# Six modulation blocks moved from TensorE to GpSimd in a two-block transformer kernel

## The reference

```python
def adaln(cond, w_mod, b_mod):
    m = jax.nn.silu(cond) @ w_mod + b_mod
    return _split(m, (D_MODEL, D_MODEL, D_MODEL))
...
sh_l, sc_l, ga_l = adaln(c, w_mod[layer], b_mod[layer])
sh_c, sc_c, ga_c = adaln(c_ctx, w_mod[layer], b_mod[layer])
h_lat = rms_norm(x_lat, g_pre[layer]) * (1 + sc_l[:, None]) + sh_l[:, None]
```

## Time and profile before

| | |
|---|---|
| runs (3) | 2313.47 us median, 2302.77 to 2314.18 |
| profiled execution | 2318.67 us, its span 2316.9 us |
| granted clock, mean | 0.985 of full |
| PE busy | 2250.4 us (97%) |
| DVE busy | 1409.2 us (61%) |
| ACT busy | 877.6 us (38%) |
| POOL busy | 10.4 us |
| ring loads | 154 x 2 MB, 7.7 us to landing |

### The profile page before, as it was taken

One profiled execution on the slowest core, in us unless ns is written; L12 is line 12 of the kernel. 1 busy time (PEld: TensorE's weight loads), 2 busy tenths in 40 slices (PEclk: granted clock), 3 DMA queues, 4 the chain that ended last, 5 costly groups with the idle time before them and its releaser, 6 DMA issues.

```text
span 2316.9 us, 34330 instructions
## 1 busy us (share of the span) xinstructions
PE 2250.4 (97%) x14514; PEld 1974.6 (85%) x14514; DVE 1409.2 (61%) x2026; ACT 877.6 (38%) x994; POOL 10.4 (0%) x23
## 2 busy tenths in 40 slices
PE   7999999999999999999999999999999997999997
PEld 7997999799889879997997568888788857999976
DVE  5556876755465568767556455666666257665564
ACT  4333474334333333652443332222434242443442
POOL 0000000000000000000000000000000000000000
PEclk9999999999999999999999999999999998999998
DMA  6555545646454544555554421111212342232331
GB/s 243 208 220 196 187 182 188 230 170 231 182 200 183 218 182 184 183 197 219 212 192 172 164 109 73 73 62 48 73 37 74 117 146 73 93 126 74 138 118 55
DMA packets 26552, 349.39 MB, mean 151 GB/s; under 512 B 2912, under 2 KB 3168, under 8 KB 5728
## 3 DMA queue, kind: packets, MB, share of 16 engines
q1 hardware_dynamic: 23888, 336.49, 39.2%
q0 software_dynamic: 2512, 10.72, 1.4%
HBM read 346.14 MB, written 1.05 MB: 150 GB/s over the span
## 4 chain that ended last, share of the span: by engine, by line
PE 87%; DVE 6%; ACT 2%; DMA 2%; DVEq 1%; issue 1%; ACTq 0%; SPq 0%
PE banks L703 12%; PE banks L708 12%; PE banks L704 12%; PE banks L792 9%; PE banks L868 9%; PE banks L926 5%; PE banks L927 5%; PE banks L930 5%; PE banks L944 2%; PE banks L940 2%; PE banks L941 2%; PE banks L1105 2%; PE banks L1106 2%; PE banks L696 2%; PE banks L1103 2%; PE banks L752 2%
## 5 line engine op out<-in xcount | busy, mean ns | idle before, releaser
L1808 DVE TENSOR_TENSOR w_lo<-ring,w_hi 128x2048 fp32r<-128x2048 f32 x290 | 662.6, 2291 | 468.9 <-ACT w_hi L1312 465.0
L1312 ACT ACTIVATE w_hi<-ring 128x2048 fp32r<-128x2048 f32 x290 | 554.8, 1917 | 705.5 <-PE banks L708 485.3
L703 PE MATMUL banks<-x_hi,w_hi 128*128 128x256 f32 x2208 | 520.4, 278 | 1.4 <-ACT arena L1406 1.4
L704 PE MATMUL banks<-x_lo,w_hi 128*128 128x256 f32 x2208 | 519.5, 277 | 0.0
L703 PEld LDWEIGHTS banks<-x_hi,w_hi 128*128 128x128 f32 x2208 | 415.5, 188 | 1.8 <-ACT arena L1406 1.8
L704 PEld LDWEIGHTS banks<-x_lo,w_hi 128*128 128x128 f32 x2208 | 415.5, 188 | 0.0
L708 PE MATMUL banks<-x_hi,w_lo 128*128 128x256 f32 x2208 | 298.3, 278 | 0.0
L708 PEld LDWEIGHTS banks<-x_hi,w_lo 128*128 128x128 f32 x2208 | 273.3, 188 | 0.4 <-DVE w_lo L1808 0.4
L1343 ACT ACTIVATE arena<-banks 128x512 f32<-128x512 f32 (+3 forms) x164 | 79.2, 498 | 443.1 <-PE banks L930 200.5
L926 PE MATMUL banks<-x_hi,w_hi 128*128 128x512 f32 (+1 forms) x656 | 237.6, 374 | 0.0
L927 PE MATMUL banks<-x_lo,w_hi 128*128 128x512 f32 (+1 forms) x656 | 228.8, 361 | 0.0
(11 more groups left out here) (322 smaller groups left out, 2800.3 us busy)
## 6 DMA issues: line engine op xcount, KB each, us to landing
ring<-weights SPq DMA_DIRECT2D x154, 2048.0 KB, 7.7
arena<-mods SPq DMA_DIRECT2D x5, 2048.0 KB, 12.2
bcast<-lnrows POOLq DMA_DIRECT2D x12, 512.0 KB, 4.9
arena<-hy_consts POOLq DMA_DIRECT2D x1, 1152.0 KB, 7.5
xrow<-x SPq DMA_DIRECT2D x1, 1024.0 KB, 4.9
arena<-hy_consts POOLq DMA_DIRECT2D x1, 1024.0 KB, 10.5
xrow<-ctx_rows POOLq DMA_DIRECT2D x1, 1024.0 KB, 5.3
out<-xrow SPq DMA_DIRECT2D x2, 512.0 KB, 2.7
```

Source lines behind the costliest of these rows:

```text
L703: nc.tensor.matmul(out, hi[:, k, t * P:(t + 1) * P], x_h[:, k, :], start=k == 0, stop=False)
L704: nc.tensor.matmul(out, hi[:, k, t * P:(t + 1) * P], x_l[:, k, :], start=False, stop=False)
L1312: nc.scalar.activation(hi, raw, ACT.Copy).then_inc(w_hi_done, 1)
L1808: v.tensor_tensor(lo, raw, hi.bitcast(F32), ALU.subtract).then_inc(w_lo_done, 1)
```

## The change

Blocks 5 to 10 leave the ring and TensorE's rows. In three of the four FFNs GpSimd loads two of them, one after the other, into `mod_w`. It multiplies the eight 128x512 pieces by the condition columns (a scalar for each partition) and adds them up in a new tile `vacc`, so that 128 partial sums per output column remain. In the turn behind the FFN, TensorE adds over the partitions: eight fp32 matmuls per block, with a piece of `vacc` as the weights and one column of ones moving, straight into the form of columns. The two steps `mod_copy` and `mod_columns` fall away for these blocks. SP's load of the next early block into `mod_w` moves from behind down block 0 to behind down block 2 and waits for GpSimd's count `vmod_done`. `vtmp` and `vacc` lie in parts of the arena that are free in an FFN.

```diff
-    return up(0) + down(0) + mix + up(1) + down(1) + (mod(5, 6, 7) if l == DEPTH - 1 else [])
+    return up(0) + down(0) + mix + up(1) + down(1)
...
-    blocks += [(("ey", j), 2) for j in range(4)] + [(("mod", m), 0) for m in (8, 9, 10)]
+    blocks += [(("ey", j), 2) for j in range(4)]
...
+FFN_MODS = {(0, 0): (5, 6), (0, 1): (7, 8), (1, 0): (9, 10)}
...
     def mod_use(n):
-        for kind in ("mrow", "mcol"):
-            uses[kind, n] = (4, count[4])
-            count[4] += 1
+        if 3 * l + n < 5:
+            for kind in ("mrow", "mcol"):
+                uses[kind, n] = (4, count[4])
+                count[4] += 1
+        if n % 2 == 0:
+            for bank, m in enumerate(FFN_MODS.get((l, n // 2), ()), 5):
+                uses["vcol", m] = (bank, count[bank])
+                count[bank] += 1
...
-                if l < DEPTH and (kind, *rest) in (("down", 0, 0), ("up", 1, 0), ("down", 1, 0)):
-                    m = 3 * l + (("down", 0, 0), ("up", 1, 0), ("down", 1, 0)).index((kind, *rest))
+                if l < DEPTH and (kind, *rest) in (("down", 0, 2), ("up", 1, 0), ("down", 1, 2)):
+                    m = 3 * l + (("down", 0, 2), ("up", 1, 0), ("down", 1, 2)).index((kind, *rest))
...
                     if kind == "up":
                         sp.wait_ge(m_done, 4 * l + 4)
+                    else:
+                        sp.wait_ge(S2["vmod_done"], 2 * (l + l + rest[0]) + 2)
                     sp.dma_start(mod_w, mods[m].rearrange("p (k n) -> p k n", k=KT)).then_inc(S2["mod_in"], 16)
...
+            def modulation(l, f, slot, k):
+
+                i = 2 * l + f
+                w = mod_w[:, k, :]
+                if k == 0:
+                    pool.wait_ge(S2["cond_done"], 1)
+                    if i:
+                        filled(pool, *mod_key("mcol", FFN_ORDER[2 * i - 2 + slot]))
+                    pool.wait_ge(S2["vmod_in"], 16 * (2 * i + slot + 1))
+                    for c in range(2):
+                        nc.gpsimd.tensor_scalar(vacc[:, slot, c, :], w, cond[:, k, c:c + 1], None, ALU.mult)
+                else:
+                    for c in range(2):
+                        nc.gpsimd.tensor_scalar(vtmp[:, c, :], w, cond[:, k, c:c + 1], None, ALU.mult)
+                    nc.gpsimd.drain()
+                    for c in range(2):
+                        nc.gpsimd.tensor_tensor(vacc[:, slot, c, :], vacc[:, slot, c, :], vtmp[:, c, :], ALU.add)
+                if k < KT - 1:
+                    nc.gpsimd.drain()
+                else:
+                    nc.gpsimd.drain().then_inc(S2["vmod_done"], 1)
...
+                    if (l, n / 2) in FFN_MODS:
+                        for slot, m in enumerate(FFN_MODS[l, n // 2]):
+                            if slot:
+                                pool.wait_ge(S2["vmod_done"], 2 * (2 * l + n // 2) + 1)
+                            elif l + n == 0:
+                                filled(pool, 0, "layer", "up", 0, 1, 0)
+                            else:
+                                filled(pool, *mod_key("mrow", 3 * l + n - 1))
+                            pool.dma_start(mod_w, mods[m].rearrange("p (k n) -> p k n", k=KT))\
+                                .then_inc(S2["vmod_in"], 16)
+                            for k in range(KT):
+                                modulation(l, n // 2, slot, k)
...
+                if n % 2 == 0 and (l, n // 2) in FFN_MODS:
+                    for slot, v_mod in enumerate(FFN_MODS[l, n // 2]):
+                        pe.wait_ge(S2["vmod_done"], 2 * (2 * l + n // 2) + slot + 1)
+                        b = take(pe, *mod_key("mcol", v_mod))
+                        for t in range(4):
+                            for c in range(2):
+                                mm = nc.tensor.matmul(banks[:, b, 2 * t + c:2 * t + c + 1],
+                                                      vacc[:, slot, c, t * P:(t + 1) * P], ones[:, 0:1],
+                                                      start=True, stop=True)
+                        mm.then_inc(full[b], 1)
```

More of the change, by code:

```diff
@@ L94, in layer_blocks @@
     down = lambda f: [(("down", f, q), 2 if 2 * q + 1 < DOWN_HALVES else 1) for q in range(W2_BLOCKS)]
-    mod = lambda *numbers: [(("mod", m), 0) for m in numbers]
     mix = []
@@ L131 @@
 BLOCK_OF, HALF_OF, HALVES = number_blocks()
+FFN_MODS = {(0, 0): (5, 6), (0, 1): (7, 8), (1, 0): (9, 10)}
+FFN_ORDER = [m for pair in FFN_MODS.values() for m in pair]
 MOD_BLOCK = {key[2]: n for key, n in BLOCK_OF.items() if key[1] == "mod"}
@@ L158, with plan_layer @@
 SLOT0_LAST = max(h for h, s in HI_SLOT.items() if s == 0 and h < FIRST_HALVES)
-def plan_layer(last):
+def plan_layer(l):
     uses, count, pair = {}, [0] * 8, [0]
+    last = l == DEPTH - 1
     def pair_use(*key):
@@ L239, in plan_banks @@
         "start": (1, in_turn(*[("turn", b, b) for b in range(4)])),
-        **{("layer", l): (1, plan_layer(l == DEPTH - 1)) for l in range(DEPTH)},
+        **{("layer", l): (1, plan_layer(l)) for l in range(DEPTH)},
         "even": (1, in_turn(
-            *[("pre", k, k) for k in range(KT)], *[(kind, m, 2 * m - 10) for m in (6, 7) for kind in ("mrow", "mcol")],
+            *[("pre", k, k) for k in range(KT)],
             *[("gg", w, h, 7) for w in range(2) for h in range(2)],
@@ L251, in plan_banks @@
         "even_y": (1, in_turn(*[("y", h, r, ((0, 1, 2, 6), (3, 4, 5, 7))[h][r]) for h in range(2) for r in range(4)])),
-        "odd": (1, in_turn(*[(kind, m, m - 8) for m in (8, 9) for kind in ("mrow", "mcol")],
-                           *[("pre", k, k) for k in range(KT)], ("mrow", 10, 2), ("mcol", 10, 2), ("gif", 3),
+        "odd": (1, in_turn(*[("pre", k, k) for k in range(KT)], ("gif", 3),
                            ("ct", 6), ("em", 7))),
@@ L360, in build @@
         mod_w = arena[:, top[0]:top[0] + BLK].rearrange("p (k n) -> p k n", k=KT)
+        vtmp = arena[:, FT * SEQ * 2 + 1024:FT * SEQ * 2 + 2048].rearrange("p (c n) -> p c n", c=2)
+        vacc = arena[:, top[0] + BLK:top[0] + BLK + 2048].rearrange("p (s c n) -> p s c n", s=2, c=2)
         th_g_at, th_g = arena_at + 4 * top[0], part(4096, 2 * KT, SEQ)
@@ L513, in mod_key @@
         def mod_key(kind, m):
+            if m in FFN_ORDER:
+                return FFN_ORDER.index(m) // 4, "layer", "vcol", m
             if m < 6:
                 return m // 3, "layer", kind, m % 3
-            return 0, "even" if m < 8 else "odd" if m < 11 else "tail", kind, m
+            return 0, "tail", kind, m
         half_keys = {h: key for key, h in HALF_OF.items()}
@@ L970, in features_ready @@
                 return lambda k: pe.wait_ge(S2["x2_split"], KT * layer + k + 1)
-            mod_row(5, range(KT))
             pe.wait_ge(S2["f_done"], 1)
@@ L984, in _ @@
                                            for t in range(2)], done=b)
-                if p == 1:
-                    mod_columns(5)
             turn_all("even", erow)
-            mod_row(6, range(KT))
-            mod_row(7, range(KT))
-            mod_columns(6)
             def even_gains(w, h):
@@ L1011, in _ @@
                         .then_inc(full[b], 1)
-                    if i == 0 and t == 0:
-                        mod_columns(7)
                     if i == 1 and t == 0:
@@ L1177, in _ @@
                     even_half(j, side)
-            mod_row(8, range(KT))
-            mod_row(9, range(KT))
-            mod_columns(8)
-            mod_columns(9)
             turn_all("odd", yrow)
-            mod_row(10, range(KT))
             pe.wait_ge(S2["gw_split"], 1)
@@ L1892, in ffn @@
                         mod_add(3 * l + 2 * f - 1)
+                        for m in FFN_MODS[0, 1] if (l, f) == (1, 0) else ():
+                            mod_add(m)
                 for q in range(DOWN_HALVES - 2):
@@ L1992, in _ @@
                         mod_add(3 * l)
+                        for m in FFN_MODS[l, 0]:
+                            mod_add(m)
                     after(l, "xb", h, 1)
@@ L2133, in _ @@
             weights_lo(HALF_OF[DEPTH, "hy", 0, 1])
-            for m in (6, 7):
-                mod_add(m)
             def hy(i, c):
@@ L2356, in _ @@
             prenorm(1, yrow)
-            for m in (8, 9):
-                mod_add(m)
-            v.drain()
             pre_gain(1)
@@ L2529, in block @@
         return m.reshape(KT, P, n).transpose(1, 0, 2).reshape(P, BLK)
-    def modulation(*numbers):
-        out.extend(block(i["w_mod_2"][m // 6][:, 512 * (m % 6):512 * (m % 6 + 1)]) for m in numbers)
     def units(m):
@@ L2565, in weight_blocks @@
         ffn(1)
-    modulation(5, 6, 7)
     return out
 def early_modulation(i):
-    return np.stack([i["w_mod_2"][0][:, 512 * m:512 * (m + 1)].reshape(KT, P, 512).transpose(1, 0, 2).reshape(P, BLK)
-                     for m in range(5)])
+    return np.stack([i["w_mod_2"][m // 6][:, 512 * (m % 6):512 * (m % 6 + 1)].reshape(KT, P, 512)
+                     .transpose(1, 0, 2).reshape(P, BLK) for m in range(11)])
```

(2 more changed lines are left out.)

13 lines of the change are left out of this document (2 added, 11 removed).

## The result

| | before | after |
|---|---|---|
| runs beside each other | 2308.40 us (2302.77 to 2328.62, 6 runs) | 2347.64 us (2344.81 to 2350.27, 6 runs) |
| profiled execution, its span | 2318.67 us, 2316.9 us | 2345.66 us, 2343.6 us |
| granted clock, mean | 0.985 | 0.971 |

The change makes the kernel slower: the ratio is 1.0157, with an interval of 1.0133 to 1.018. The profiled spans differ by 26.7 us, the medians by 39.2 us; the profiled execution of before lies 10 us above the median of its runs here, which accounts for most of the difference.

The account below looks back on a forecast made before the run. TensorE, busy 97% of the span, was taken to bound the kernel. Terms -8.0 - 8.5 - 9.0 + 7.2 = -18.3 us, from an adjusted 2313.5, gave 2295 us if FFNs ran as before; range 2285 to 2334.

Parts of the forecast that it names:

- The step that failed: GpSimd in the FFNs: 60 operations of 128x512 at 1.0 us each, 60 us, within the 1.63 us each allowed in the first.
- upper bound of 1.3 us: GpSimd's average operation if each operand and the result cost a memset's pass: multiply 1.1 us, add 1.6.
- Rival 1: FFNs: GpSimd and DVE hold each other up, 46 us lost, 28 us slower in all, 2341 us; chance 0.26.
- The deadline: SP's queue: SP must pass its wait for GpSimd by 161 in the first FFN, 600.5 in the second.
- The second block: Modulation matmuls removed from TensorE at the second block's layers: gains of 8.0, 8.5 and 9.0 us.
- block 5: Start of the second block: row matmuls of 6.96 us and columns of 1.05 us go, all moves forward, -8.0 us.
- blocks 6 and 7: Before the first Hyena tile: 9.2 us won, 7.5 after reduced clock, plus 1.0 for later columns: -8.5 us.
- Blocks 8 to 10: From their first row matmuls to the first mLSTM head tile: -9.0 us, bounds 6.5 and 11.5.
- Rival 3: Second block: removed work was mostly cover as TensorE waits for ACT; gain only 9 us, 2304 us; chance 0.09.
- The turns: Three turns behind FFNs get 16 one-column matmuls each, 3.73 us, less 4.0 us of covered waits: +7.2 us.
- a slower DVE alone does no harm: FFN up phases: w_lo is ready several us before its use, so slower DVE costs nothing by itself.
- Rival 2: Milder holding: operations take 1.6 to 1.85 us, only the first FFN loses, up to 13 us; middle 2303; chance 0.19.

Follow-up runs that it names:

- the merged kernel: Each GpSimd pair of 512 columns merged into one instruction of 1,024, against the kernel with broadcast multiply and original wait: 2310.53 us, ratio 0.9974.
- the kernels with one repair each: Changed kernel with only SP's wait moved behind down block 4: 2314.68 us, ratio 1.000; or with only the broadcast multiply: 2316.58 us, ratio 1.0019.

## Why the prediction was wrong

It forecast 2295 us with a range of 2285 to 2334; the kernel takes 2347.6, outside of it, and "slower" had a chance of 0.24.

**The step that failed** is "I take 1.0, nearer the upper since the engine has to read as well: 60 us". Its upper bound of 1.3 us was too low even for GpSimd alone: 32 x 1.55 + 28 x 1.24 = 84 us, 1.41 each. Beside DVE it was 2.06 us in the first FFN and, by the same working, 2.18 in the second (487.65 to 639.69, less 21.5 us of loads). The bound counted each operand as a memset's pass, which puts the multiply at 1.1 us; it took 1.55, more than the add with its two inputs. The loads went the other way, 9.3 + 9.5 = 18.8 us where the sum had 24.4; without that SP would have passed another 5.6 us late. The Trainium skill's page "GPSIMD Engine Reference", section on elementwise cycle accounting, gives 769 ns for a tight loop of 512 elements; the measured multiply by a column scalar is twice that.

**Rival 1 came true in its mechanism, and its numbers are in part luck.** It said 22 us in the first FFN and 12 in each of the others; the trace has 21.7, 13.2 and 7.3. The rival meant 46 us of waiting, though, where the trace has 34.3, some 9 of reduced clock behind the stalls, and the wandering pace, which put 4 us on FFN 2 and took 4 off the difference of FFN 3. It decides "from 1.93 us per operation beside DVE, or 0.89 us alone"; they are 2.06 and 1.41. Set against the profiled execution it gives 2318.7 + 28 = 2346.7, and 2345.66 was measured. Its 2.17 us also rested on a wrong pair: 1.0 us alone, standing still for 54% of the time. In fact GpSimd is longer alone (1.41 us) and held up less (some 0.6 us of the 2.06), and DVE is held up in turn. That the two come near each other, 2.17 and 2.06, is luck. Its chance of 0.26 was too low: one unknown price carried the outcome, and the rival needed only 0.89 us of it.

**The deadline was right.** SP had to pass by 161 and passed 18.6 us late; TensorE lost 20.7. In FFN 2, which started 30 us later, the deadline of 600.5 becomes 630.5, SP passed at 639.69, and 4.6 us were lost, part of the 9 being covered by a slow stretch of TensorE. In FFN 3, which started 45.9 us later than before, at 698.29, the second one's deadline counted from the FFN's start gives 840.0; SP passed at 848.27, and 9.0 us were lost. The experiments bear it out: SP's pass less the stall is 158.9 in the first FFN of the changed kernel, 159.1 with the broadcast multiply and 159.2 with work in the first FFN only, and the merged kernel, which passes at 154.38, has no such stall; behind down block 4 it is 186.42 - 13.09 = 173.3 and 175.67 - 2.07 = 173.6. So the deadline was 159 where the prediction had 161. What the step missed is the clock behind a stall, some 3 us each.

**The second block was right**: -8.2 for block 5 (forecast -8.0) and -8.2 for blocks 6 and 7 (forecast -8.5). Term by term: -9.2 up to the start of the first Hyena tile, as forecast; in that tile 24 matmuls take 7.80 us, from 1385.93 to 1393.73, where they took 5.79 before (1352.33 to 1358.12), since they now stand behind the wait, and ten of them start 0.43 us apart: 2.0 us of reduced clock, where 1.7 had been allowed for; and -1.0 for the columns of block 7. Blocks 8 to 10 give -9.7 (forecast -9.0). "So TensorE idles 9.9 us" before the first Hyena tile: the wait there is 9.90. Rival 3, the removed work as cover, is out.

**The turns were right** in the changed kernel: +7.6 against +7.2. That "a slower DVE alone does no harm" held as well: the kernel with the later wait and the cheaper multiply has a mean w_lo of 2743 ns in the first FFN and one wait of 2.1 us there, which SP's late pass explains. It stops holding for the merged instructions, where the first short waits for w_lo appear.

**Rival 2**, the milder loss, is in kind what the kernels with one repair each show: 13.1 and 12.2 us of stall, in the first FFN alone. Their times, 2314.7 and 2316.6, lie above its 2296 to 2308.

## What to carry to other kernels

Work handed to an idle engine has a deadline wherever a shared queue waits for it. Work out that deadline, then the price per instruction at which it is missed; if that price is near your guess and no row shows the instruction, measure it before anything else, alone and beside the neighbour's real instructions. If the deadline is missed, first try the other form of the same instruction and a later place for the wait: together they turned +1.6% into -0.4% here, with the same work on the same engines. Where two engines hold each other up, look at both: the forms that were quicker for GpSimd were dearer for DVE. A wait for slow work in a queue of its own may be worth trying too, which no run here did: each microsecond by which GpSimd was late held back weights that had nothing to do with it.

## What the runs showed of the hardware that was not expected

GpSimd's multiply of 128x512 by a column scalar took 1.55 us, by an immediate 1.47, as a two-input multiply with a broadcast column 1.02; an add of two inputs took 1.24. Both forms with a single tensor as input were dearer than both with two.

A GpSimd instruction and a DVE one with two SBUF inputs took turns, one for one: rounds of 5.90 us became 11.93, and DVE's 2.29 us became 2.85. Some 0.7 us of each pair still overlapped. A DVE cast (one SBUF input) doubled, from 428 to 852 ns, while GpSimd lost 6%; a DVE instruction that reads PSUM and one SBUF input changed neither.

After a stall of 4.6 us TensorE's granted clock was 0.79 in the next 15 us, after 9.0 us 0.82, after 20.7 us 0.82: in these cases the cost of a stall was its length and about 3 us. After the wait of 9.9 us ahead of the first Hyena tile it was 2.0 us.
